# Padded sampled tiles and a moved feature sum in the gated recurrence of a one-core decoder kernel

## The chip, the cores and the metric

The kernel runs on one core of a Trainium2 chip. The metric is the device time of one execution in microseconds. Three executions of the kernel before took 2487.93, 2488.98 and 2489.5 us, so the median is 2488.98 us. TensorE (PE in the rows) multiplies, VectorE (DVE) and ScalarE (ACT) do elementwise work, GpSimd (POOL) only makes constants here, and SyncE (SP) issues most DMAs.

## The reference

A decoder trunk of two layers runs over 512 prompt tokens and 64 sampled tokens (8 sequences of 8). Layer 0 mixes with a gated linear recurrence of 8 heads with a 128 x 128 state each; layer 1 mixes with a diagonal state-space layer. Gated feed-forward blocks stand before and after each mixer. Cut to the recurrence:

```python
proj = h @ w_in                       # q, f, i, g of 1024 features each
fg = lbf + (1 - lbf) * sigmoid(f);  log_f = log(fg);  k = (1 - lbf) * sigmoid(-f)
# per token and head: S_t = diag(f_t) S_(t-1) + k_t v_t^T,  o_t = S_t^T q_t
o, s_T = chunk_scan(heads(q), heads(k), heads(i), heads(log_f), s0)
o = o * rsqrt(mean(o * o, axis=-1) + EPS) * gnorm
return (o * silu(g)) @ w_out, s_T
```

## The kernel before

All activations lie with features on the 128 partitions and the 576 tokens (512 prompt, then 64 sampled) along the row. A product of float32 quality is made of three products, h_hi w_hi, h_lo w_hi and h_hi w_lo, each in two halves of 288 tokens (line 1687). The halves w_hi and w_lo are made on ScalarE (`split`, line 657) and on VectorE (`rest`, line 1024).

The recurrence is the phase `hgrn_in`. It goes head by head; a step of the program projects head n and, between those matmuls, works on head m = n - 1. The 32 blocks of six matmuls that project head n are cut at the numbers in `cuts`, and after each cut stands a piece of head m. The pieces, in the order of TensorE, are:

- eight levels (0 to 7) of score matmuls. `level` multiplies k by q for four prompt tiles of 128 tokens (line 1822, a float32 matmul is two instructions in the trace) and, for levels 0 to 3, for the 64 sampled tokens (line 1824, 64 columns of k). VectorE's `level` multiplies q, k and the decay row (lines 1381 to 1383), which releases TensorE's next level, and then copies the scores under a mask (lines 1389 and 1393). Even levels use bank 4 of PSUM, odd ones bank 5, the sampled parts banks 6 and 7;
- `v_turned`, behind level 4, and `k_turned`, three blocks behind level 7: five transposes each into banks 6 and 7 (line 1657), copied by ScalarE to `v_tok` and `k_tok` (lines 803 and 804);
- `chunk_adds`, the k v products of the four chunks (line 1849), which VectorE's `chain` turns to the chunk states (lines 1411 and 1417);
- `tail`, behind the last block: sampled k v products, 64 rows deep and 512 columns wide, into banks 6 and 7 (line 1857); the prompt outputs in bank 5 (lines 1864 and 1866); the sampled outputs in bank 4 (line 1868, 64 rows deep, and line 1871, eight matmuls 8 columns wide); and last the sum over features of the squared outputs (line 1878), which needs ScalarE's squares (lines 830 and 831) in the tile `sq`.

ScalarE takes the root of those sums (line 833), VectorE inverts it in four quarters (`invert`, line 1443) in the next step, and `normalise` (line 1449) and `o_rest` (line 1454) finish the output of that head. VectorE also scales the projections as they leave PSUM (line 1050 by way of `scaled`), and adds the sampled k v products to the decayed states (line 1427) and gates the outputs (lines 1433 and 1435, which end with the semaphore `on_done`). Each engine runs its queue in program order; semaphores alone connect them. The last step projects no head: the first blocks of the phase `hgrn_out` stand between its levels, two behind each of the first six cuts.

## Time and profile before

| what | value |
|---|---|
| median of three executions | 2488.98 us |
| the profiled execution, its own time | 2480.59 us |
| its span, first to last instruction | 2478.8 us |
| TensorE busy | 2337.1 us (94%) |
| VectorE busy | 1220.8 us (49%) |
| ScalarE busy | 701.8 us (28%) |
| mean granted TensorE clock | 0.975 |
| DMA | 211.08 MB, mean 85 GB/s |

The profiled execution is 8.4 us (0.34%) shorter than the median of the three timed ones, and its span is 1.8 us shorter than its own time. Busy time counts an engine's instructions; TensorE's are pipelined, so that neighbouring rows overlap, and the distance between starts tells what one costs. An arrow in a row names what released the instruction after an idle stretch.

### The profile page before, as it was taken

The numbers are of one execution on the slowest core, as the hardware profiler recorded it, in microseconds if no ns is written. First come the engines' busy times: TensorE is split into PE (matmuls) and PEld (weight loads), VectorE is DVE, ScalarE is ACT, GpSimd is POOL, SyncE is SP. The second block draws the span as 40 slices with busy tenths as digits, with TensorE's granted clock in tenths as the row PEclk, the third lists the DMA queues.
The fourth block names the chain that finished last, engine by engine and source line by source line (L and its number), as shares of the span: only waits on it lengthen the run. The fifth ranks groups of instructions, "written<-read, shape, count | busy, mean of one in ns | idle before, by whom it ended". The sixth has DMA issues, their size and how long they took to land.

```text
span 2478.8 us, 42614 instructions
## 1 busy us (share of the span) xinstructions
PE 2337.1 (94%) x17438; PEld 2294.5 (93%) x17438; DVE 1220.8 (49%) x1730; ACT 701.8 (28%) x878; POOL 2.7 (0%) x15
## 2 busy tenths in 40 slices
PE   6999999899999979999999999999955999999998
PEld 6999999889999879999999999999945999999998
DVE  5755544756667665432344443243377434433333
ACT  3222222334434333221222322122234432221223
POOL 0000000000000000000000000000000000000000
PEclk9999999999999999999999999999967999999999
DMA  4223432432231115323422332322333233223322
GB/s 125 82 65 109 122 85 64 121 108 70 73 84 52 44 53 135 96 69 93 113 80 85 89 85 64 105 69 66 87 107 102 74 85 86 80 73 84 85 70 70
DMA packets 398495, 211.08 MB, mean 85 GB/s; under 512 B 23025, under 2 KB 393922, under 8 KB 398402
## 3 DMA queue, kind: packets, MB, share of 16 engines
q1 hardware_dynamic: 387666, 198.03, 28.8%
q10 hardware_dynamic: 10736, 11.77, 1.5%
q8 instruction: 63, 1.03, 0.2%
q14 instruction: 30, 0.25, 0.0%
HBM read 193.01 MB, written 20.94 MB: 86 GB/s over the span
## 4 chain that ended last, share of the span: by engine, by line
PE 87%; DVE 7%; issue 2%; ACT 2%; DMA 0%; ACTq 0%; SPq 0%; DVEq 0%
PE ps L1687 78%; PE ps L1822 2%; PE ps L1657 2%; DVE rstd L1045 1%; PE ps L1857 1%; PE ps L1871 1%; PE ps L1986 1%; PE ps L1987 1%; DVE w_lo L1024 0%; ACT w_hi L657 0%; PE ps L1878 0%; PE ps L1765 0%; DVE sq L1547 0%; PE ps L1864 0%; DVE sq L1550 0%
## 5 line engine op out<-in xcount | busy, mean ns | idle before, releaser
L1687 PE MATMUL ps<-h_hi,w_hi 128*128 128x288 f32 x3328 | 723.4, 299 | 14.5 <-DVE t_a L1050 11.6
L1687 PE MATMUL ps<-h_hi,w_lo 128*128 128x288 f32 x3328 | 713.9, 296 | 0.0
L1687 PE MATMUL ps<-h_lo,w_hi 128*128 128x288 f32 x3328 | 713.5, 296 | 0.0
L1687 PEld LDWEIGHTS ps<-h_hi,w_hi 128*128 128x128 f32 x3328 | 536.6, 189 | 20.2 <-issue 6.5
L1687 PEld LDWEIGHTS ps<-h_hi,w_lo 128*128 128x128 f32 x3328 | 537.4, 189 | 0.0
L1687 PEld LDWEIGHTS ps<-h_lo,w_hi 128*128 128x128 f32 x3328 | 537.3, 189 | 0.0
L1024 DVE TENSOR_TENSOR w_lo<-w_raw,w_hi 128x2048 fp32r<-128x2048 f32 (+3 forms) x184 | 369.8, 2010 | 123.8 <-ACT w_hi L657 122.1
L657 ACT ACTIVATE w_hi<-w_raw 128x2048 fp32r<-128x2048 f32 (+3 forms) x184 | 309.5, 1682 | 216.8 <-PE ps L1687 204.6
L1687 PE MATMUL ps<-g_hi,w_hi 128*128 128x288 f32 x1408 | 304.7, 298 | 0.0
L1687 PE MATMUL ps<-g_lo,w_hi 128*128 128x288 f32 x1408 | 303.2, 297 | 0.0
L1687 PE MATMUL ps<-g_hi,w_lo 128*128 128x288 f32 x1408 | 303.0, 297 | 0.0
L1050 DVE TENSOR_TENSOR t_b<-ps,rstd 128x576 f32<-128x576 f32 x88 | 66.6, 757 | 435.9 <-PE ps L1687 435.9
L1687 PEld LDWEIGHTS ps<-g_hi,w_hi 128*128 128x128 f32 x1408 | 228.7, 190 | 0.0
L1687 PEld LDWEIGHTS ps<-g_hi,w_lo 128*128 128x128 f32 x1408 | 228.6, 190 | 0.0
L1687 PEld LDWEIGHTS ps<-g_lo,w_hi 128*128 128x128 f32 x1408 | 228.5, 190 | 0.0
L723 ACT ACTIVATE g_hi<-t_g 128x576 f32 (+1 forms) x88 | 60.3, 685 | 527.4 <-DVE t_g L1283 527.4
L1328 DVE SCALAR_TENSOR_TENSOR x<-ps,x 128x576 f32<-128x576 f32 (+1 forms) x72 | 54.5, 757 | 247.9 <-PE ps L1687 247.8
L720 ACT ACTIVATE t_s<-t_a 128x576 f32<-128x576 f32 x88 | 60.3, 686 | 326.9 <-DVE t_a L1050 326.9
L1285 DVE TENSOR_TENSOR g_lo<-t_g,g_hi 128x576 f32 (+1 forms) x88 | 66.7, 758 | 79.8 <-ACT g_hi L723 79.8
L1050 DVE TENSOR_TENSOR t_a<-ps,rstd 128x576 f32<-128x576 f32 x88 | 66.2, 752 | 21.8 <-PE ps L1687 21.8
L688 ACT ACTIVATE h_hi<-x,vec 128x576 fp32r<-128x576 f32 (+1 forms) x40 | 31.0, 775 | 153.2 <-DVE x L1328 93.0
L1283 DVE TENSOR_TENSOR t_g<-t_b,t_s 128x576 f32<-128x576 f32 x88 | 66.8, 759 | 15.2 <-DVE t_b L1050 12.0
(301 smaller groups left out, 1860.5 us busy)
## 6 DMA issues: line engine op xcount, KB each, us to landing
w_raw<-in_ffn_w_in_dram SPq DMA_DIRECT2D x176, 512.0 KB, 4.8
w_raw<-in_ffn_w_out_dram SPq DMA_DIRECT2D x64, 384.0 KB, 3.7
w_raw<-in_ffn_w_out_dram SPq DMA_DIRECT2D x64, 320.0 KB, 3.4
w_raw<-in_hgrn_w_in_dram SPq DMA_DIRECT2D x32, 512.0 KB, 5.3
w_raw<-in_s_w_glu_dram SPq DMA_DIRECT2D x16, 512.0 KB, 4.7
wb_d<-wb_st ACTq DMA_DIRECT2D x8, 512.0 KB, 2.7
wc_d<-c_pow ACTq DMA_DIRECT2D x8, 512.0 KB, 3.5
s_in<-in_state_hgrn_dram SPq DMA_DIRECT2D x8, 512.0 KB, 3.9
```

Source lines behind the costliest of these rows:

```text
L657: nc.scalar.activation(w_hi[j][:, 0:ph.size], w_raw[j][:, 0:ph.size], ACT.Copy).then_inc(w_hi_done[j], 1)
L688: nc.scalar.activation(cols(h_hi, m), cols(x, m), ACT.Copy, scale=vec[:, bass.ds(m + gain, 1)])\
L720: nc.scalar.activation(t_s[:], t_a[:], ACT.Silu).then_inc(silu_done, 1)
L723: nc.scalar.activation(cols(g_hi, i * 2 + j), t_g[:], ACT.Copy).then_inc(g_hi_done, 1)
L1024: V.tensor_tensor(w_lo[j][:, 0:n], w_raw[j][:, 0:n], f32(w_hi[j][:, 0:n]), ALU.subtract)\
L1050: return V.tensor_tensor(halves(dst), pair(s), halves(rstd[:]), ALU.mult)
L1283: V.tensor_tensor(t_g[:], t_b[:], t_s[:], ALU.mult).then_inc(g_full, 1)
L1285: V.tensor_tensor(cols(g_lo, i * 2 + j), t_g[:], f32(cols(g_hi, i * 2 + j)), ALU.subtract)\
L1328: V.scalar_tensor_tensor(out=halves(cols(x, m)), in0=pair(j), scalar=scale, in1=halves(cols(x, m)), op0=ALU.mult, op1=ALU.add).then_inc(fr ...
L1657: return M.transpose(out, t, ident[0:n, 0:n])
L1687: ins = M.matmul(ps[:, 2 * s + h, 0:HALF], w[j][:, at:at + P], v[:, k, h * HALF:(h + 1) * HALF], start=k == 0 and n == 0, stop=k == ph.kt ...
L1822: ins = M.matmul(ps[:, 4 + n % 2, at], k_t[b][:, at], q_t[b][:, at], start=True, stop=True)
```

## The change

Four tiles get 128 entries where they had 64 for the sampled tokens: `k_t` and `v_t` are 640 wide with zeros in the last 64 columns, `own_seq` and `v_seq` have 128 rows. With them every matmul and transpose on sampled tokens uses 128 rows and 128 columns of weights: the sampled scores, the fifth transpose, the sampled k v products and the first sampled output. ScalarE copies both transposed banks in one instruction of 640 columns. The sampled k v products move from the tail to just behind `chunk_adds`. The feature sums of a head move from the end of its tail to behind level 4 of the next head; `v_turned` moves from behind level 4 to behind level 5, and waits for the root of those sums. On ScalarE the root of the head before stands behind the two sigmoids of the next step instead of ahead of the weight split. On VectorE the first inverted quarter moves from behind level 1 to behind level 5, and the second from behind level 4 to behind the scaling of v. Level 0 of the next head waits for `s_out_done` (line 1427's) instead of the root.

```diff
-    own_seq = sb("own_seq", [SAMPLE, DEC_BATCH])
+    own_seq = sb("own_seq", [P, DEC_BATCH])
...
-    k_t = [sb(f"k_t{b}", [P, T]) for b in range(2)]
+    k_pad = [sb(f"k_t{b}", [P, T_PAD]) for b in range(2)]
+    k_t = [k[:, 0:T] for k in k_pad]
...
-    v_seq = sb("v_seq", [SAMPLE, DEC_BATCH, P])
+    v_seq = sb("v_seq", [P, DEC_BATCH, P])
...
...
-                    nc.scalar.activation(dst[:, 0:CHUNKS, :].rearrange("p c q -> p (c q)"), ps[:, 6, :], ACT.Copy)
-                    nc.scalar.activation(dst[0:SAMPLE, CHUNKS, :], ps[0:SAMPLE, 7, 0:P], ACT.Copy).then_inc(done, 1)
+                    turned_both = ps[:, 6:8, :].rearrange("p b q -> p (b q)")[:, 0:T_PAD]
+                    nc.scalar.activation(dst[:].rearrange("p c q -> p (c q)"), turned_both, ACT.Copy).then_inc(done, 1)
...
-                    act.wait_ge(r_full, m + 1)
+
+                def head_root(head):
+                    act.wait_ge(r_full, head + 1)
                     nc.scalar.activation(halves(sq[:]), ps[:, 6:8, 0:HALF], ACT.Sqrt, scale=1.0 / P, bias=eps_t[:])\
...
+                    if n is not None:
+                        project_f(n, b)
+                    if before is not None:
+                        head_root(before)
...
...
-                    invert(before, 0)
                     if n is not None:
                         rest(ph, 1, n)
...
-                    invert(before, 1)
-                    if m is not None:
                         level(m, mb, 5)
+                    invert(before, 0)
...
                         take(v_t[:], 0, n, 1)
+                        invert(before, 1)
                         if last:
                             rest(PH[n_ph + 1], 0, 0)
...
+                    if n is None:
+                        invert(before, 1)
                     invert(before, 2)
...
...
-                            pe.wait_ge(osd_done, m)
+                            pe.wait_ge(s_out_done, m)
...
-                        ins = M.matmul(ps[0:SAMPLE, 6 + n % 2, 0:SAMPLE], k_t[b][:, SEQ:T], q_t[b][:, SEQ:T],
+                        ins = M.matmul(ps[:, 6 + n % 2, 0:SAMPLE], k_pad[b][:, SEQ:T_PAD], q_t[b][:, SEQ:T],
...
-                    turn(ps[0:SAMPLE, 7, 0:P], t[:, SEQ:T]).then_inc(done, 1)
+                    turn(ps[:, 7, 0:P], t[:, SEQ:T_PAD]).then_inc(done, 1)
...
+                    if not isinstance(m, int) or m:
+                        pe.wait_ge(osd_done, m)
+                    turned(v_pad, vt_full)
...
-                        ins = M.matmul(ps[:, 6 + h, :], k_tok[0:SAMPLE, CHUNKS, :], v, start=True, stop=True)
+                        ins = M.matmul(ps[:, 6 + h, :], k_tok[:, CHUNKS, :], v, start=True, stop=True)
...
-                    M.matmul(ps[:, 4, 0:SAMPLE], v_tok[0:SAMPLE, CHUNKS, :], score[0:SAMPLE, SEQ:T], start=True, stop=False)
+                    M.matmul(ps[:, 4, 0:SAMPLE], v_tok[:, CHUNKS, :], score[:, SEQ:T], start=True, stop=False)
...
-                    pe.wait_ge(osq_done, m + 1)
-                    pe.wait_ge(s_out_done, m + 1)
+                def sums(count):
+
+                    pe.wait_ge(osq_done, count)
+                    pe.wait_ge(s_out_done, count)
...
-                            if at == SAMPLE_LEVELS:
+                            if at == SAMPLE_LEVELS and (not isinstance(m, int) or m):
+                                pe.wait_ge(sc_read, m * LEVELS + SAMPLE_LEVELS)
+                                sums(m)
+                            if at == SAMPLE_LEVELS + 1:
                                 v_turned(m)
...
                                 chunk_adds(m)
+                                sampled_adds(m)
...
+                sums(HEADS)
```

Three places of the engines' order are shown, of a step in the loop over heads. First VectorE, from the mask copy of level 6 to the inversion behind level 7, before:

```order
L1389 COPY_PREDICATED score<-masks,ps 128x512
L1398 REGISTER_ALU
L1050 TENSOR_TENSOR v_t<-ps,rstd 128x576
L1022 REGISTER_ALU
L1024 TENSOR_TENSOR w_lo_56<-w_raw_52,w_hi_54 128x2048
L1363 REGISTER_ALU
L1381 TENSOR_TENSOR q_t_99<-q_t_99,e_t 128x4x64
L1382 TENSOR_TENSOR k_t_101<-k_t_101,e_t 128x4x64
L1383 TENSOR_TENSOR e_t<-e_t 128x4
L1389 COPY_PREDICATED score<-masks,ps 128x512
L1443 RECIPROCAL o_rs<-sq 128x144 x2
```

And the same stretch now (v scaled by line 1058, `rest` in line 1032, the level in lines 1391 to 1399, `invert` in line 1454):

```order
L1399 COPY_PREDICATED score<-masks,ps 128x512
L1409 REGISTER_ALU
L1058 TENSOR_TENSOR v_t<-ps,rstd 128x576
L1454 RECIPROCAL o_rs<-sq 128x144
L1030 REGISTER_ALU
L1032 TENSOR_TENSOR w_lo_56<-w_raw_52,w_hi_54 128x2048
L1373 REGISTER_ALU
L1391 TENSOR_TENSOR q_t_99<-q_t_99,e_t 128x4x64
L1392 TENSOR_TENSOR k_t_101<-k_t_101,e_t 128x4x64
L1393 TENSOR_TENSOR e_t<-e_t 128x4
L1399 COPY_PREDICATED score<-masks,ps 128x512
L1454 RECIPROCAL o_rs<-sq 128x144 x2
```

One inversion of 128x144 now stands between the scaling of v and the weight remainder w_lo, and so ahead of the multiplications of level 7.

Second TensorE, the end of a step, from the last projection row to the end of the tail, before (line 1857 the sampled adds, 1878 the feature sums):

```order
L1687 MATMUL ps<-h_lo,w_hi_55 128x288 x2
L1687 MATMUL ps<-h_hi,w_lo_57 128x288 x2
L1857 MATMUL ps<-v_seq,k_tok 128x512 x2
L1864 MATMUL ps<-score,v_tok 128x128 x2
L1866 MATMUL ps<-q_t_98,s_chunk 128x128
L1864 MATMUL ps<-score,v_tok 128x128
L1866 MATMUL ps<-q_t_98,s_chunk 128x128
L1864 MATMUL ps<-score,v_tok 128x128
L1866 MATMUL ps<-q_t_98,s_chunk 128x128
L1868 MATMUL ps<-score,v_tok 128x64
L1871 MATMUL ps<-q_t_98,s_in_115 128x8 x8
L1878 MATMUL ps<-sq,ones 128x288 x2
```

Now the sampled adds (line 1871) follow the chunk adds (line 1863), two blocks earlier:

```order
L1699 MATMUL ps<-h_hi,w_lo_57 128x288 x2
L1863 MATMUL ps<-v_tok,k_tok 128x128 x4
L1871 MATMUL ps<-v_seq,k_tok 128x512 x2
L1699 MATMUL ps<-h_hi,w_hi_55 128x288 x2
L1699 MATMUL ps<-h_lo,w_hi_55 128x288 x2
```

The tail now begins behind the last projection row and ends without the sums:

```order
L1699 MATMUL ps<-h_hi,w_lo_57 128x288 x2
L1880 MATMUL ps<-score,v_tok 128x128 x2
L1882 MATMUL ps<-q_t_98,s_chunk 128x128
L1880 MATMUL ps<-score,v_tok 128x128
L1882 MATMUL ps<-q_t_98,s_chunk 128x128
L1880 MATMUL ps<-score,v_tok 128x128
L1882 MATMUL ps<-q_t_98,s_chunk 128x128
L1884 MATMUL ps<-score,v_tok 128x64
L1887 MATMUL ps<-q_t_98,s_in_115 128x8 x8
```

The sums stand behind level 4 of the next head (line 1896), with the second weight tile's blocks behind them:

```order
L1829 REGISTER_ALU
L1834 MATMUL ps<-q_t_99,k_t_101 128x128 x4
L1896 MATMUL ps<-sq,ones 128x288 x2
L1692 REGISTER_ALU
L1699 MATMUL ps<-h_hi,w_hi_55 128x288 x2
L1699 MATMUL ps<-h_lo,w_hi_55 128x288 x2
```

Third ScalarE, from the gate's silu of one step to the sigmoid of the next, before (root in line 833, weight split in line 657):

```order
L797 ACTIVATE s_g_102<-pre 128x576
L830 ACTIVATE sq<-ps 128x512
L831 ACTIVATE sq<-ps 128x64
L833 ACT_TABLE_LOAD
L833 ACTIVATE sq<-ps,eps_t 128x576
L657 ACTIVATE w_hi_55<-w_raw_53 128x2048
L789 ISA
L790 ACT_TABLE_LOAD
L790 ACTIVATE k_t_101<-pre 128x576
```

And the start of a step now (sigmoids in lines 793 and 796, root in line 838, the copy of the transposed v in line 807):

```order
L793 ACTIVATE k_t_100<-pre 128x576
L795 ISA
L796 ACTIVATE f_t<-pre 128x576
L838 ACT_TABLE_LOAD
L838 ACTIVATE sq<-ps,eps_t 128x576
L807 ACTIVATE v_tok<-ps 128x640
L659 ISA
L660 ACTIVATE w_hi_54<-w_raw_52 128x2048
L815 ACTIVATE v_seq<-v_tok,own_seq 128x128 x8
```

The root with its table load stands between the second sigmoid and the copy of the transposed v.

## Rows read from the trace of the kernel before

**Rows 1.** The page: the chain that ended last, share of the span by engine.
```profile
PE 87%; DVE 7%; issue 2%; ACT 2%; DMA 0%; ACTq 0%; SPq 0%; DVEq 0%
```

**Rows 2.** Windows over two heads: engine busy times, granted clock, DMA share.
```profile
678.00:767.00 89.00, 87.02 (x644) 81.72 (x644) 59.95 (x112) 35.59 (x66) 0.00 (x0) 1.00 0.26 72
```

**Rows 3.** Waits from 500 to 900 us: total, times, longest.
```profile
ACT k_tok L803 <- PE ps L1657: 38.3, 8, 5.8
...
PE ps L1878 <- ACT sq L831: 6.4, 8, 0.8
...
PEld ps L1857 <- issue: 5.1, 23, 0.2
```

**Rows 4.** Timeline of TensorE, end of a head: start, length, instruction; next head's sums.
```profile
715.68 0.43 PE L1687 MATMUL ps<-h_hi,w_lo 128*128 128x288 f32 x2
716.04 1.98 PE L1857 MATMUL ps<-v_seq,k_tok 64*128 64x512 f32 x4
...
720.07 1.95 PE L1871 MATMUL ps<-q_t,s_in 128*128 128x8 f32 x16
722.83 1.24 PE L1878 MATMUL ps<-sq,ones 128*128 128x288 f32 x4 [0.80 <-ACT sq L831]
...
724.16 0.42 PE L1687 MATMUL ps<-h_lo,w_hi 128*128 128x288 f32 x2
...
767.14 1.24 PE L1878 MATMUL ps<-sq,ones 128*128 128x288 f32 x4 [0.80 <-ACT sq L831]
```

**Rows 5.** Timeline of TensorE, level 0 with and level 5 without sampled scores.
```profile
726.27 1.05 PE L1822 MATMUL ps<-q_t,k_t 128*128 128x128 f32 x8
727.25 0.33 PE L1824 MATMUL ps<-q_t,k_t 128*64 128x64 f32 x2
...
727.88 0.42 PE L1687 MATMUL ps<-h_lo,w_hi 128*128 128x288 f32 x2
...
745.80 1.05 PE L1822 MATMUL ps<-q_t,k_t 128*128 128x128 f32 x8
...
746.96 0.43 PE L1687 MATMUL ps<-h_lo,w_hi 128*128 128x288 f32 x2
```

**Rows 6.** Transposes of v by form, and TensorE's timeline of level 4 around them.
```profile
L1657 PE MATMUL ps<-ident,v_t x40: 272/273/273, 565.6 to 872.7; 128*128 128x128 f32 x32, 128*64 128x128 f32 x8
...
741.98 1.05 PE L1822 MATMUL ps<-q_t,k_t 128*128 128x128 f32 x8
...
743.68 0.30 PE L1687 MATMUL ps<-h_lo,w_hi 128*128 128x288 f32 x1
```

**Rows 7.** Timeline of VectorE around the tail and level 7, and TensorE's transpose of k.
```profile
723.57 0.27 DVE L1435 SCALAR_TENSOR_TENSOR ssq<-ps,vec,s_g 128x64 f32<-128x64 f32 x1
...
755.32 0.16 DVE L1383 TENSOR_TENSOR e_t<-e_t 128x4 f32<-128x4 f32 x1
...
756.01 1.95 DVE L1443 RECIPROCAL o_rs<-sq 128x144 f32<-128x144 f32 x2
...
755.64 0.71 PE L1657 MATMUL ps<-ident,k_t 128*128 128x128 f32 x5
```

**Rows 8.** Timeline of ScalarE: squares, table load, root, second sigmoid.
```profile
722.55 0.22 ACT L831 ACTIVATE sq<-ps 128x64 f32<-128x64 f32 x1
722.79 1.28 ACT L833 ACT_TABLE_LOAD   x1
...
724.10 0.74 ACT L833 ACTIVATE sq<-ps,eps_t 128x576 f32<-128x576 f32 x1
...
743.63 0.67 ACT L793 ACTIVATE f_t<-pre 128x576 f32<-128x576 f32 x1
```

**Rows 9.** Timeline of the last head, TensorE and VectorE.
```profile
866.76 0.53 PE L1687 MATMUL ps<-o_hi,w_hi 128*128 128x288 f32 x2 [1.12 <-DVE w_lo L1024]
...
884.89 0.35 DVE L1417 SCALAR_TENSOR_TENSOR s_end<-s_chunk,e_t,ps 128x128 f32<-128x128 f32 x1
...
885.39 0.68 PE L1864 MATMUL ps<-score,v_tok 128*128 128x128 f32 x4
```

More of the change, by code:

```diff
@@ L39 @@
 HALF = T // 2
+T_PAD = SEQ + P
 BANK = 512
@@ L202, in build_trunk @@
     q_t = [sb(f"q_t{b}", [P, T]) for b in range(2)]
-    k_t = [sb(f"k_t{b}", [P, T]) for b in range(2)]
+    k_pad = [sb(f"k_t{b}", [P, T_PAD]) for b in range(2)]
+    k_t = [k[:, 0:T] for k in k_pad]
     s_g = [sb(f"s_g{b}", [P, T]) for b in range(2)]
     f_t = sb("f_t", [P, T])
-    v_t = sb("v_t", [P, T])
+    v_pad = sb("v_t", [P, T_PAD])
+    v_t = v_pad[:, 0:T]
     pre = sb("pre", [P, T])
@@ L811, in own_values @@
                     for s in range(DEC_BATCH):
-                        ins = nc.scalar.activation(v_seq[:, s, :], v_tok[0:SAMPLE, CHUNKS, :], ACT.Copy,
+                        ins = nc.scalar.activation(v_seq[:, s, :], v_tok[:, CHUNKS, :], ACT.Copy,
                                                    scale=own_seq[:, s:s + 1])
@@ L824, in decayed, with squares @@
                     ins.then_inc(decay_done, 1)
-                def tail(m):
+                def squares(m):
                     act.wait_ge(o_full, m + 1)
@@ L848, in step @@
                             split(ph, 1, n, ph, n - 1)
-                        project_f(n, b)
                     elif m is not None:
                         split(PH[n_ph + 1], 1, 0, ph, None)
+                    if n is not None:
+                        project_f(n, b)
+                    if before is not None:
+                        head_root(before)
                     if m is not None:
@@ L870, in step @@
                     if m is not None:
-                        tail(m)
+                        squares(m)
                 step(0, 0, None, None, None)
@@ L1357, in hgrn @@
                 reciprocal(1)
+                for t in (k_pad[0], k_pad[1], v_pad):
+                    V.memset(t[:, T:T_PAD], 0.0)
                 link(V.memset(score[:], 0.0))
@@ L1392, in level @@
                     if n < SAMPLE_LEVELS:
-                        ins = V.copy_predicated(score[0:SAMPLE, SEQ:T], masks_s[:, n, :], ps[0:SAMPLE, 6 + n % 2, 0:SAMPLE])
+                        ins = V.copy_predicated(score[0:SAMPLE, SEQ:T], masks_s[:, n, :],
+                                                ps[0:SAMPLE, 6 + n % 2, 0:SAMPLE])
                     ins.then_inc(sc_read, 1)
@@ L1835, in v_turned @@
                     pe.wait_ge(sc_read, m * LEVELS + SAMPLE_LEVELS)
-                    turned(v_t, vt_full)
+                    if not isinstance(m, int) or m:
+                        pe.wait_ge(osd_done, m)
+                    turned(v_pad, vt_full)
                 def k_turned(m, b):
@@ L1841, in k_turned @@
                     pe.wait_ge(vtok_done, m + 1)
-                    turned(k_t[b], kt_full)
+                    turned(k_pad[b], kt_full)
                 def chunk_adds(m):
@@ L1850, in chunk_adds, with sampled_adds @@
                     ins.then_inc(kvp_full, 1)
-                def tail(m, b):
+                def sampled_adds(m):
                     pe.wait_ge(vseq_done, m + 1)
@@ L1856, in tail @@
                         v = v_seq[:, 4 * h:4 * h + 4, :].rearrange("p b v -> p (b v)")
-                        ins = M.matmul(ps[:, 6 + h, :], k_tok[0:SAMPLE, CHUNKS, :], v, start=True, stop=True)
+                        ins = M.matmul(ps[:, 6 + h, :], k_tok[:, CHUNKS, :], v, start=True, stop=True)
                     ins.then_inc(kvs_full, 1)
+                def tail(m, b):
                     pe.wait_ge(sc_read, m * LEVELS + LEVELS)
```

## The prediction

> **What bounds the kernel now.** I read the page first: TensorE is on 87% of the chain that ended last [rows 1], in a span of 2478.8 us (the table above). So only what shortens TensorE's own queue, or a wait of it, counts. The windows over two heads of the recurrence show TensorE busy 87.02 of 89 us at a full granted clock of 1.00, VectorE 59.95 and ScalarE 35.59 [rows 2]: here, too, TensorE is the bound, and its stalls are few but repeated, once or more in each period of 44.31 us (two starts of the feature sums) [rows 4]. The waits name them: 8 times TensorE waits for the squares before the feature sums, and 23 times its weight loads sit idle around line 1857 with no engine named ("issue") [rows 3]. The timeline then gives their price.
>
> The unit of price: 16 projection matmuls stand between 724.16 [rows 4] and 726.27 [rows 5], 0.132 us each. Level 5 takes 1.16 us from its first matmul to the second pair of projections [rows 5]; less two projections that is 0.112 us for each of its eight instructions.
>
> **The change, part by part**
>
> *Sampled scores, levels 0 to 3.* Level 0 takes 1.61 us on the same measure, 0.45 more than level 5, for two instructions with 64 columns of weights [rows 5]. At the pace above two would cost 0.22. With all 128 columns of weights I take 0.22, because 16 matmuls of line 1871 with full weights and only 8 moving columns keep about the same pace (1.95 us for all) [rows 4]. Saved: 0.23 a level, 0.9 a head. Bounds: nothing, or the whole 0.45 were the two free.
>
> *Sampled k v products and first sampled output.* From 715.68 to 720.07 stand two projections, four of line 1857, fourteen of lines 1864 and 1866 and two of line 1868: 4.39 us [rows 4]. Without a gap: 0.26, four at 0.43, sixteen at 0.112 (1.79), together 3.77. The 0.43 is an estimate by width: the sums of 288 columns take 0.24 each (below), 512 columns are 1.78 times that; the block's own 1.98 for four [rows 4] caps it at 0.5. Saved: 0.62, of which about 0.4 lies at line 1857 and 0.23 at line 1868. With the levels, 1.55 a head. That line 1857 now stands two blocks earlier is free: it needs the copy of k, for which `chunk_adds` waits anyway, and the eight copies to `v_seq`, and ScalarE, done with those, was idle until the transposed k came, 38.3 us in eight heads [rows 3].
>
> *Transposes.* Eight of the 40 for v have 64 columns of weights. Level 4 with its five transposes takes 1.70 us, 0.54 more than level 5, or 0.109 for each, the narrow one included [rows 5, 6]. Nothing to save. The Trainium skill, page "TensorEngine Tiling (Array Packing)", section "Key Properties", says that changing the tiling mode drains the engine. The score rows agree with it; the transpose rows don't show it, and the measurement decides. By the rule the 16 narrow transposes would save about 0.23 each, 3.7 us more.
>
> *The feature sums.* From 720.07 to 724.16 is 4.09 us [rows 4]; with projections directly behind the tail it would be 16 x 0.112 + 2 x 0.132 = 2.05. So 2.04 leaves the tail. In place the four sums take 1.07 (722.83 to 724.16 less two projections), the restart after the wait included [rows 4]. Without about 0.1 for the restart that is 0.24 each; behind level 4 I take 1.0, between 0.97 and 1.07. Their input is ready 20 us before (the squares end at 722.77, level 4 at 742.9) [rows 6, 8], and the wait for the mask copy of level 3 stood at the same spot before, ahead of the transposes of v, without idle time.
>
> *What now follows the tail.* Level 0 waits for `on_done`. It comes at 723.84, 3.77 us after 720.07 [rows 4, 7]. Level 0 would start 16 x 0.112 + 18 x 0.132 = 4.17 us after it: 0.4 to spare, so no stall in the loop. In the last step only 12 projections stand there, 3.37 us, so it waits about 0.5.
>
> *The root.* On ScalarE it now follows the second sigmoid, which ends at 744.30, 2.32 us after level 4 starts at 741.98 [rows 6, 8]. The table load takes 1.28, and the root 0.74 [rows 8]: finished 4.4 after the start of level 4. TensorE reaches the transposes of v after 0.9 + 1.0 + 18 x 0.132 + 0.9 = 5.2. It is hidden, with 0.8 to spare. The chip shows no more than the load itself: the square ends at 722.77, the load starts at 722.79 and ends at 724.07, the root starts at 724.10 [rows 8]. The Trainium skill, "ScalarE: Activation LUTs", section "What ACT_TABLE_LOAD costs", adds a drain of 1.38 us to the load; by that the root would come 0.6 us late.
>
> *The inversions, the cost of the change.* One quarter takes 0.98 us (1.95 for two) [rows 7]. The first, now behind level 5, falls into idle time of VectorE. The second stands ahead of the weight remainder and of level 7's multiplications. Those end at 755.48, and TensorE's transposes of k, which wait for them, start at 755.64 [rows 7]. There is at most 0.16 us of slack. With 0.98 more ahead, TensorE waits about 0.9, plus some hundredths for a first matmul after idle time: I take 0.94, between 0.8 and 1.1. Behind it, chunk adds, VectorE's chain and the tail shift together. VectorE's chain is still in time for the tail: in the last head, with no projections between, it ends 0.15 ahead of it (885.24 against 885.39) [rows 9], and in the loop two blocks of projections, 1.6 us, stand there as cover.
>
> *The sum.* Heads 1 to 6, one period each: 1.55 + 2.04 - 1.0 - 0.94 = 1.65, six times 9.9 us. Head 0 has no earlier head, so no sums and no inversions in it: 1.55. The last head gains 1.15 (levels and first output), 1.54 at its start (2.04 for the sums gone, 0.5 for the wait for `on_done`), and about 0.55 of the wait of 1.12 for w_lo, since an inversion no longer stands ahead of it [rows 9]. Against that the chain of VectorE decides: its slack was 0.15. It gets 0.46 later by the sums less the transposes moved, 0.98 by a third inversion behind level 7, and by an estimated 0.3 for the first behind level 5, the part that idle time does not cover: 1.6 after the slack. Net 1.65 for the last head. The last feature sums stay exposed. Sum: 9.9 + 1.55 + 1.65 = 13.1 us. The profiled execution would go from 2480.6 to 2467.5; it stands 8.4 us under the median of the runs, so I take the gain from the median: 2489.0 - 13.1 = **2475.9 us**. The mask tiles, the zero fills (three memsets before the first head) and the copy of 640 columns in one are worth less than 0.5 us in all, off the chain.
>
> **The rivals**
>
> *No stall at the transposes of k* (10%): if the weight remainder or the multiplications get their place earlier than I see, for instance because VectorE's scaling of v comes earlier in the step. For it: VectorE is idle a third of the time. Against: its stretch from v to level 7 is dense. Time: 6 x 0.94 = 5.6 less, 2470.3.
>
> *The narrow transposes pay a gap of their own* (3%): 16 of them at the 0.23 of a score level, 3.7 us more saved, 2472.2. Against it stands the pace of 0.109. That is what the Trainium skill's tiling page (above) implies.
>
> *The root comes late* (6%): if a switch of tables in mid-queue costs twice the load's 1.28, TensorE waits 0.5 (1.28 less the 0.8 to spare) and a restart of 0.1, six times: 3.6 us, 2479.5. Against it the 0.03 us between load and root. The drain on the Trainium skill's page on ScalarE would be such a second cost.
>
> *The padding does nothing* (8%): the gaps come from something other than the 64-wide form, a change of bank or of source. Then 1.55 is lost seven times and 1.15 once, 12.0 us: 2487.9, no change. Against it: line 1871 and line 1868 write the same bank and the gap stands between them all the same.
>
> *Slower* (5%): the root is now waited for in three queues, by TensorE ahead of the transposes of v, by ScalarE's copies behind it, by VectorE's inversion ahead of the gates. Each microsecond beyond the 0.8 to spare costs six. To lose over 0.2% (5 us) it must first eat 13.1, so it decides from 18.1 / 6 + 0.8 = 3.8 us late. At 4.5 us late: 2475.9 + 6 x 3.7 = 2498. Against it: the sigmoids end 2.3 us behind the start of level 4 now, and nothing new stands ahead of them.
>
> **How the numbers follow.** The forecast has 68%. A measurement of this kernel can tell about 0.2% from no change, 5 us. The forecast and the first three rivals are faster by more (87%), the padding rival is the same (8%), the last slower (5%). The forecast's own bounds are 0.8 to 1.1 for the stall (1.8 us over six heads), 0.97 to 1.07 for the sums (0.6) and 1 us for the last head: 2474 to 2478. The range reaches from the first rival to beyond the late root, with the 0.3% between profile and median in mind: 2470 to 2482 (it leaves out the last two).
>
> **What would show it.** In the profile after: a period of 42.66 us between heads where two starts of line 1871's block or of the sums stand 44.31 apart now; no "issue" waits at the sampled adds; the sampled score pair at 0.22; no idle time at the sums; a new wait of TensorE, transposes of k for VectorE's e_t, of about 0.9 us, six times; none at the transposes of v. Wrong would be: waits for the root at the transposes of v, a wait at level 0 for the gated outputs in the loop, or a granted clock under 1.00 in the recurrence.

## The result, and the profile after

| | median | range | executions | profiled execution | its span |
|---|---|---|---|---|---|
| before | 2489.24 us | 2487.93 to 2491.3 | 4 | 2480.59 us | 2478.8 us |
| changed | 2468.94 us | 2468.46 to 2469.75 | 4 | 2469.75 us | 2468.0 us |

The ratio is 0.9918 (95% interval 0.9904 to 0.9932): the changed kernel is 0.8%, 20.3 us, faster. Forecast were 2475.9 us and a range from 2470 to 2482, so the kernel came out 7.0 us below the forecast and 1 us below the range. The direction was right, the size too small.

The page of the changed kernel, busy times and the chain that ended last (to be read beside the table of before and [rows 1]):

```profile
PE 2327.8 (94%) x17438; PEld 2294.4 (93%) x17438; DVE 1220.7 (49%) x1733; ACT 702.0 (28%) x862; POOL 2.8 (0%) x15
...
PE 86%; DVE 8%; issue 3%; ACT 2%; DMA 0%; ACTq 0%; SPq 0%; DVEq 0%
```

TensorE still bounds the kernel, busy 9.3 us less; VectorE and ScalarE have the work that they had. Where the bound lost time is seen in its waits. This is TensorE in the loop over heads of the changed kernel, from 560 to 840 us (line waited at, releaser: total, times, longest). It is the only wait there:

```profile
PE ps L1669 <- DVE e_t L1393: 3.2, 5, 0.7
```

And the same view from 840 to 900 us, the last head and what follows it (left out: two waits of line 1699's products, for o_lo and w_lo):

```profile
...
PE ps L1834 <- DVE e_t L1393: 1.5, 2, 1.1
PE ps L1669 <- DVE e_t L1393: 0.9, 1, 0.9
PE ps L1863 <- ACT k_tok L807: 0.9, 1, 0.9
PE ps L1896 <- ACT sq L834: 0.8, 1, 0.8
PE ps L1834 <- DVE ssq L1446: 0.2, 1, 0.2
```

In the loop the six waits for the squares are gone (8 in all in [rows 3], one is left, after the last head), and the new wait that was forecast stands there, transposes of k for VectorE's e_t. The row gives 0.64 us each, idle time behind modelled ends of matmuls; by starts it costs 0.86 (`inv_behind`, below). It comes five times, not six, because the last step of the loop has only half a weight remainder ahead of level 7 (VectorE's line 1032 with 1024 columns in 1.16 us, in the other steps 2048 in 2.23). There is no wait at the transposes of v, so the root is never late, and none at level 0 inside the loop.

One sign that was forecast did not come. The weight loads of the sampled adds still sit idle with no engine named, 4.4 us in 16 times from 500 to 900 us, where [rows 3] have 5.1 in 23. So that row was not the price of the 64-wide form:

```profile
PEld ps L1871 <- issue: 4.4, 16, 0.5
```

The timeline of TensorE in one head of the changed kernel shows the pieces (start, length, instruction):

```profile
693.18 1.05 PE L1834 MATMUL ps<-q_t,k_t 128*128 128x128 f32 x8
694.07 1.14 PE L1896 MATMUL ps<-sq,ones 128*128 128x288 f32 x4
694.83 0.64 PE L1699 MATMUL ps<-h_hi,w_hi 128*128 128x288 f32 x2
695.31 0.42 PE L1699 MATMUL ps<-h_lo,w_hi 128*128 128x288 f32 x2
...
698.33 0.71 PE L1669 MATMUL ps<-ident,v_t 128*128 128x128 f32 x5
...
707.56 0.43 PE L1699 MATMUL ps<-h_hi,w_lo 128*128 128x288 f32 x2
708.61 0.77 PE L1669 MATMUL ps<-ident,k_t 128*128 128x128 f32 x5 [0.62 <-DVE e_t L1393]
...
711.69 1.88 PE L1871 MATMUL ps<-v_seq,k_tok 128*128 128x512 f32 x4
713.01 0.83 PE L1699 MATMUL ps<-h_hi,w_hi 128*128 128x288 f32 x2
713.68 0.42 PE L1699 MATMUL ps<-h_lo,w_hi 128*128 128x288 f32 x2
...
715.00 0.61 PE L1880 MATMUL ps<-score,v_tok 128*128 128x128 f32 x4
...
716.73 1.90 PE L1887 MATMUL ps<-q_t,s_in 128*128 128x8 f32 x16
718.49 0.50 PE L1699 MATMUL ps<-h_hi,w_hi 128*128 128x288 f32 x2
...
720.95 1.05 PE L1834 MATMUL ps<-q_t,k_t 128*128 128x128 f32 x8
721.84 0.33 PE L1836 MATMUL ps<-q_t,k_t 128*128 128x64 f32 x2
...
722.33 0.42 PE L1699 MATMUL ps<-h_lo,w_hi 128*128 128x288 f32 x2
```

Level 0 takes 1.38 us from its first matmul to the second pair of projections, against 1.61 [rows 5]: 0.23 saved. The sums take 1.24 (694.07 to 695.31) less two projections, 0.98. The projections stand 1.76 us behind the start of line 1887's block, where in [rows 4] the sums follow it after 2.76. The sampled adds occupy 711.69 to 713.68 less two projections, 1.73 or four times 0.43; the fourteen instructions of the prompt outputs and the two of the first sampled output 715.00 to 716.73, 1.73.

ScalarE's timeline at the place of the moved root (the second sigmoid, the table load, the root, and the copy of the transposed v), to be read beside [rows 8]:

```profile
694.83 0.67 ACT L796 ACTIVATE f_t<-pre 128x576 f32<-128x576 f32 x1
695.52 1.28 ACT L838 ACT_TABLE_LOAD   x1
...
696.81 0.74 ACT L838 ACTIVATE sq<-ps,eps_t 128x576 f32<-128x576 f32 x1
...
699.23 0.71 ACT L807 ACTIVATE v_tok<-ps 128x640 f32<-128x640 f32 x1 [1.68 <-PE ps L1669]
```

The root ends at 697.55, 0.78 us ahead of the transposes of v. That is the 0.8 to spare of the forecast, with no second cost at the switch of tables: 0.02 us from sigmoid to load and 0.01 from load to root.

**The time, piece by piece.** I cut the span at S0 (the first matmul on the scores of head 0) and at the start of the last matmul of the sampled output of each head. The last column is a further execution of before, profiled later (below). Its own time, 2490.57 us, is that of an ordinary execution.

| piece, us | before, the profile of the forecast | changed | before, profiled again |
|---|---|---|---|
| start to S0 | 549.0 | 552.4 | 552.0 |
| head 0 | 39.8 | 38.2 | 39.8 |
| heads 1 to 6, six periods | 265.9 | 254.8 | 265.9 |
| last head | 34.45 | 32.9 | 39.8 |
| to the end | 1589.7 | 1589.7 | 1591.3 |
| span | 2478.8 | 2468.0 | 2488.8 |

The last matmuls of the last head can be read in the group of line 1887's matmuls of the changed kernel (instructions: shortest, median, longest ns, first and last start):

```profile
L1887 PE MATMUL ps<-q_t,s_in x128: 228/256/256, 588.9 to 878.3; 128*128 128x8 f32 x128
```

and in the same group of `before_again`:

```profile
L1871 PE MATMUL ps<-q_t,s_in x128: 256/256/277, 590.1 to 897.5; 128*128 128x8 f32 x128
```

Between the first two columns the recurrence is 14.3 us shorter (1.6 + 11.1 + 1.6), where 13.1 were forecast. Between the last two it is 19.6; the 5.3 us between these two numbers lie in the last head of before alone. That is most of the missing gain, and it is not in the change's sum but in its base.

### The profile page after: what moved, and what is told of

It is laid out like the page before. It is cut to its first block, busy times and chain, and to the rows that moved or that the text cites. A ratio compares the mean times of both kernels' runs of the same rounds, so it can differ in the third digit from the quotient of the medians.

```text
span 2468.0 us, 42601 instructions
## 1 busy us (share of the span) xinstructions
PE 2327.8 (94%) x17438; PEld 2294.4 (93%) x17438; DVE 1220.7 (49%) x1733; ACT 702.0 (28%) x862; POOL 2.8 (0%) x15
## 4 chain that ended last, share of the span: by engine, by line
PE 86%; DVE 8%; issue 3%; ACT 2%; DMA 0%; ACTq 0%; SPq 0%; DVEq 0%
PE ps L1699 78%; PE ps L1834 2%; PE ps L1669 2%; DVE rstd L1053 1%; PE ps L1871 1%; PE ps L1887 1%; DVE w_lo L1032 1%; PE ps L2009 1%; PE ps L2010 0%; ACT w_hi L660 0%; PE ps L1777 0%; DVE o_rs L1454 0%; DVE sq L1559 0%; DVE sq L1562 0%; PE ps L1896 0%
## 5 line engine op out<-in xcount | busy, mean ns | idle before, releaser
L2009 PE MATMUL ps<-wi,u_lift 128*72 128x128 f32 x128 | 28.2, 307 | 49.0 <-ACT s_v L952 28.5
```

The costliest lines, as they stand in the source:

```text
L2009: M.matmul(out, u_lift[:, G_CT * ct + g, :], wi[ct % 2][:, g], start=True, stop=False)
```

## The experiments

In all of them `ones` and `zero` are tiles that matmuls without use read: in kernels with `fill`, their result is overwritten, or they add a product with zeros to a bank, and no value of the output changes.

### The kernel before, again, with all padding alone, with the moves alone

`before_again` is the kernel before without an edit.

> The kernel before, unchanged, for the spans of its own executions. In the two traces the recurrence (first score level to the last sampled output) is 14.3 us shorter after the change, but the timed medians differ by 20.3 us, and the one profiled execution of before was 8.4 us under its timed ones. Theory A: the change is worth 14 us in the recurrence, and the rest is a part outside it that varied in the executions of before; then the spans of this kernel spread from about 2479 to 2488 us, and a trace of a longer one shows the recurrence unchanged at 340.2 us and the extra time elsewhere. Theory B: the recurrence itself usually takes some 6 us longer than the first trace showed: then a longer execution shows periods over 44.3 us.

Measured: 2489.43 us (ratio 1.0005, 0.9995 to 1.0015). Neither theory fits as it was written. The recurrence is longer, as theory B has it, but its periods are unchanged at 44.31 us: the last head took 39.8 us where the first profile had 34.45. The trace of `turn_only` (below), which differs from before by its narrow transposes alone, has the same last head, 39.76 us at a granted clock of 0.83. The windows over the last head and the 32 us behind it (busy times by engine, granted clock, DMA), in the first profile of before:

```profile
855.00:889.50 34.50, 28.77 (x202) 25.22 (x202) 22.41 (x48) 10.69 (x27) 0.00 (x0) 1.00 0.05 16
889.50:921.50 32.00, 22.30 (x138) 21.52 (x139) 17.78 (x22) 9.38 (x14) 0.00 (x0) 0.84 0.17 50
```

In `before_again`:

```profile
858.00:898.00 40.00, 34.23 (x202) 29.02 (x202) 22.57 (x48) 10.87 (x27) 0.00 (x0) 0.83 0.05 14
898.00:930.00 32.00, 23.06 (x128) 21.91 (x129) 17.21 (x22) 8.81 (x13) 0.00 (x0) 0.73 0.13 39
```

In the changed kernel:

```profile
845.60:878.50 32.90, 28.98 (x203) 25.44 (x202) 22.34 (x48) 10.44 (x24) 0.00 (x0) 0.95 0.06 16
878.50:910.50 32.00, 22.59 (x137) 21.79 (x137) 17.78 (x22) 9.10 (x14) 0.00 (x0) 0.79 0.16 48
```

The same 202 instructions of before are granted 1.00 in one execution and 0.83 in the other. The timeline of TensorE in `before_again` shows where:

```profile
879.40 1.16 PE L1822 MATMUL ps<-q_t,k_t 128*128 128x128 f32 x8 [0.94 <-DVE e_t L1383]
881.49 2.07 PE L1822 MATMUL ps<-q_t,k_t 128*128 128x128 f32 x8 [0.93 <-DVE e_t L1383]
884.49 1.33 PE L1657 MATMUL ps<-ident,k_t 128*128 128x128 f32 x5 [0.93 <-DVE e_t L1383]
...
888.67 3.78 PE L1857 MATMUL ps<-v_seq,k_tok 64*128 64x512 f32 x4
```

Level 6 (879.40) still takes 1.16 us. From level 7 (881.49) on the matmuls run at the lower of the two levels, 1.2 instead of 2.4 GHz: eight instructions in 2.07 us, and line 1857's block in 3.78 instead of 1.98 [rows 4]. What precedes is the stretch in which TensorE has no projections left and waits 0.9 us for VectorE ahead of levels 6 and 7. In the first profile the same waits stand in the same places, and level 7 takes 1.16 us.

`pad_only` has every padding of the diff, `own_seq`, `v_seq`, `k_pad`, `v_pad` and the copy in one, with the order of before. `move_only` has the order of the changed kernel, with all tiles of 64 as before (its sampled instructions keep the rows and columns that are taken away below).

```diff
 pad_only, against before
-    ins = M.matmul(ps[0:SAMPLE, 6 + n % 2, 0:SAMPLE], k_t[b][:, SEQ:T], q_t[b][:, SEQ:T],
+    ins = M.matmul(ps[:, 6 + n % 2, 0:SAMPLE], k_pad[b][:, SEQ:T_PAD], q_t[b][:, SEQ:T],
...
 move_only, against the changed kernel
-    ins = M.matmul(ps[:, 6 + h, :], k_tok[:, CHUNKS, :], v, start=True, stop=True)
+    ins = M.matmul(ps[:, 6 + h, :], k_tok[0:SAMPLE, CHUNKS, :], v, start=True, stop=True)
```

> All four tiles padded, all instructions in the order of before. Theory of the prediction: 0.9 us a head at the score levels, 0.4 at the sampled adds and 0.25 at the first sampled output: the period falls from 44.31 to 42.75 us, the time by about 12 us. Rival (the gaps belong to a change of bank or source, not to the 64-wide form): period 44.3, time as before.

> The order of after, the four tiles and their copies unpadded as before. Theory: the sums leave a wait of 1.04 us a head behind and the moved inversion makes a new one of 0.9 us, so the period stays near 44.2 us and the time falls by about 2 us, most of it at the last two heads. Rival: the new wait is smaller without the padding, since TensorE is slower by 0.9 us in levels 0 to 3, and the moves are worth 5 us or more.

Measured: `move_only` 2486.33 us (0.9991, 0.9981 to 1.0), its period 44.19 us as expected. `pad_only` 2484.99 us (0.9989, 0.9979 to 0.9998), and its period 44.4 to 44.6, not 42.75: missed. The windows of `pad_only` around the end of a head:

```profile
586.00:592.40 6.40, 5.60 (x38) 4.53 (x37) 2.22 (x3) 1.75 (x4) 0.00 (x0) 1.00 0.31 92
592.40:596.00 3.60, 3.60 (x14) 3.15 (x13) 0.70 (x2) 2.86 (x3) 0.00 (x0) 0.53 0.86 253
596.00:600.00 4.00, 4.00 (x34) 4.00 (x34) 1.50 (x3) 1.89 (x2) 0.00 (x0) 1.00 0.63 171
```

And its timeline of TensorE there:

```profile
589.38 1.90 PE L1876 MATMUL ps<-q_t,s_in 128*128 128x8 f32 x16
592.08 1.95 PE L1883 MATMUL ps<-sq,ones 128*128 128x288 f32 x4 [0.80 <-ACT sq L834]
...
594.30 0.68 PE L1692 MATMUL ps<-h_lo,w_hi 128*128 128x288 f32 x2
...
596.07 0.42 PE L1692 MATMUL ps<-h_hi,w_lo 128*128 128x288 f32 x2
```

Behind eight matmuls (sixteen instructions) of 8 moving columns and a wait of 0.80 us, the clock falls to half for about 3.5 us in each head. A pair of projections takes 0.68 instead of 0.42. That is what the padding had saved, given back. Against 2488.41 us of before on that chip, the moves alone are worth 2.1 us and the padding alone 3.4 of the 20. Set beside the changed kernel, `move_only` prices the padding in the order in which no such wait is left: the period goes from 44.19 to 42.60, 1.59 us, where 1.55 were reckoned.

The last head is slow in both. It takes 38.3 us in `pad_only`, at 0.82, and 37.9 in `move_only`:

```profile
854.70:892.60 37.90, 34.41 (x204) 29.14 (x203) 22.43 (x48) 10.65 (x26) 0.00 (x0) 0.82 0.05 14
```

So neither half of the change by itself takes the half clock out of the last head.

### The padding, with the wait filled

`pad_fill` puts four matmuls of 0.22 us into the wait of `pad_only`.

```diff
+                    fill(4, more)
                     pe.wait_ge(osq_done, m + 1)
```

> The padded tiles in the order of before, and in each head's tail, where TensorE waits for ScalarE's squares, four float32 matmuls of 128 columns (0.9 us) whose result nothing reads, into a free bank. Theory (the padding alone was eaten by TensorE's clock, which its trace shows at half for 3.4 us at the end of each head): with the wait filled the clock stays at full, the period falls from 44.5 to 42.75 us and the time to about 12 us under before. Rival (something else lengthens each head of the padded kernel by 1.8 us): the period stays at 44.5 us.

Measured: 2473.25 us (0.9932, 0.9915 to 0.9948). The window over one period of it:

```profile
592.00:635.00 43.00, 43.00 (x333) 41.61 (x331) 30.01 (x57) 17.55 (x31) 0.00 (x0) 1.00 0.27 76
```

The clock is whole, and the period 42.96 us: 1.35 less than before's 44.31, of 1.55 forecast for the padding. The fills fit into the wait, for the feature sums start 2.74 us behind the block of line 1884 here and 2.75 behind line 1871's in before. What is missing lies at level 3, 0.26 us: VectorE's multiplications, which have the first inversion and a weight remainder ahead of them in this order, now end just too late for it. So the padding does what was reckoned, and the half clock hid it. The moves, which take both the wait for the squares and this inversion out of the way, are what lets it be seen. The time fell by more than the 12 us expected, 16.8 us under the runs of before beside it (2490.01). Against the trace of `before_again`, 1.6 of it lie in head 0, 8.1 in the six periods, 2.9 in the last head (36.94 us, at 0.86) and 3.9 behind it.

### The narrow transposes alone

`turn_only` pads the fifth transpose and copies 640 columns in one, and nothing else.

```diff
-    turn(ps[0:SAMPLE, 7, 0:P], t[:, SEQ:T]).then_inc(done, 1)
+    turn(ps[:, 7, 0:P], t[:, SEQ:T_PAD]).then_inc(done, 1)
```

> Before with the fifth transpose alone padded to 128 columns, and the copy of both banks in one instruction of 640 columns. Prediction's reading of the rows: nothing to save, the period stays at 44.31 us. Rival (the narrow transposes pay a gap too): period 43.85 us. A single look, read by its period.

Measured, in a single execution: 2488.3 us, period 44.32 against 44.31. A 64-wide transpose among wide ones costs nothing here, and the rival that gave it 0.23 is refuted.

### The stall at the transposes of k

`inv_behind` is the changed kernel with the second inversion behind level 7, out of the way of the multiplications.

```diff
                         take(v_t[:], 0, n, 1)
-                        invert(before, 1)
...
                         level(m, mb, 7)
-                    if n is None:
-                        invert(before, 1)
+                    invert(before, 1)
```

> After, with VectorE's second inversion moved from ahead of the weight remainder to behind level 7. Theory: the wait of TensorE for the multiplications of level 7 (0.9 us, five heads) goes, and VectorE's chain still ends ahead of the tail: 4 to 5 us faster than after, period 41.7 us. Rival: the chain, with three inversions ahead of it, becomes what the tail waits for, and nothing is gained.

Measured: 2464.08 us (0.9905, 0.9888 to 0.9921), period 41.74 against 42.60. In the waits of its TensorE from 500 to 900 us the row on e_t keeps the last head's wait alone:

```profile
PE ps L1667 <- DVE e_t L1393: 0.9, 1, 0.9
```

So the stall costs 0.86 us a head (0.94 forecast) and the inversion ahead of level 7 is its cause. Its last head is longer, 34.0 us instead of 32.9, and the window on it has a granted clock of 0.90, with the eight instructions of line 1861's chunk adds in 2.07 us. By the ratios (0.9905 against 0.9918) the whole kernel gains about 3 us, not the 4 to 5 expected, and the two intervals overlap; the period is what shows the effect.

### What the last head of before costs at half clock

`before_fill` is the kernel before, with three matmuls of zeros (of 0.22 us each) ahead of levels 6 and 7, the transposes of k and the chunk adds of the last head only.

```diff
+                        if n is None and 6 <= at < 10:
+                            fill(3)
```

> The kernel before, with three float32 matmuls of zeros behind each of the last four cuts of the last head, added to an open sum, so that they change no value; they stand where TensorE waits 0.9 us for VectorE. Theory (in ordinary executions of before the last head runs half of its time at half clock, 39.8 us instead of 34.5): with those waits filled the last head takes 34 to 35 us and the time falls by 5 to 6 us, to about 2483. Rival: the last head is slow for the tail's narrow matmuls or for another reason, and the time stays at 2488.

Measured: 2480.13 us (0.9964, 0.995 to 0.9978), 9.9 us under the runs of before beside it (2490.01): more than expected, and about the time of the first profiled execution of before (2480.59). Its timeline of TensorE between levels 6 and 7:

```profile
879.91 0.83 PE L1775 MATMUL ps<-ident,zero 128*128 128x128 f32 x6
881.00 1.16 PE L1830 MATMUL ps<-q_t,k_t 128*128 128x128 f32 x8 [0.26 <-DVE e_t L1385]
```

The wait of 0.93 ahead of level 7 is now 0.26, with other work in it, and its eight instructions take 1.16 us instead of 2.07. The last head took 34.46, as in the first profile, and what follows it 1586.7 instead of 1591.3. So, trace against trace, 5.3 us of the gain lie in the last head and 4.6 behind it, where two traces of the changed kernel alone differ by 2.5 (1589.7 and 1587.2). The first is shown; of the second, no run tells how much is the fills' work.

`after_fill` makes the same edit in the changed kernel; `after_again` is that kernel without an edit, on the same chip.

> The changed kernel with matmuls of zeros in the waits of the last head (three behind each of the last four cuts), as in the filled kernel of before, where they were worth 9.9 us. Theory (the change already took the half clock out of the last head): 1 to 2 us faster than after, 2467 to 2468. Rival (after pays for the half clock like before): 5 us or more.

> The changed kernel once more, for a second trace of its last head and more executions. Theory: the median stays at 2469 with little spread, the last head takes 33 us nearly all at full clock. Rival (the first trace of after was lucky, as the first of before was): a last head of 36 us or more and executions up to 2475.

Measured: 2467.56 (0.9921, 0.9904 to 0.9937) and 2466.76 us (0.9916, 0.9899 to 0.9932), last heads 32.69 and 32.91. The fills bring nothing here, not even the 1 to 2 us expected. The timeline of the changed kernel's last head shows why. First the sampled adds and what follows them, in the changed kernel:

```profile
871.56 3.49 PE L1871 MATMUL ps<-v_seq,k_tok 128*128 128x512 f32 x4
874.89 0.61 PE L1880 MATMUL ps<-score,v_tok 128*128 128x128 f32 x4
```

And the same two in `after_shift` (below), whose last head has a clock of 1.00:

```profile
873.90 1.88 PE L1879 MATMUL ps<-v_seq,k_tok 128*128 128x512 f32 x4
876.99 0.68 PE L1888 MATMUL ps<-score,v_tok 128*128 128x128 f32 x4 [1.20 <-DVE s_end L1430]
```

The changed kernel has half clock too, in the sampled adds, 3.49 instead of 1.88 us. But at full clock TensorE waits there 1.20 us for the end of VectorE's chain of chunk states, so that the outputs start 3.09 us behind the adds instead of 3.33. (`after_fill` has that wait too, 1.21 us.) Here the half clock costs about 0.2 us, because it falls where VectorE is late in any case.

### Is it the design of the change, or the moment?

Each of these two has eight matmuls, 1.8 us, put ahead of the last head and is otherwise before or the changed kernel.

```diff
+                    if n is None:
+                        fill(8, True)
                     for at, cut in enumerate(cuts):
```

> The kernel before with eight float32 matmuls (1.8 us of dense work, result read by nothing) ahead of the last head's first block. If the length of the last head (39.8 us, half of it at half clock) hangs on when its thin stretch comes, it may fall to 34.5 plus 1.8 and the time falls by 3 us or more; if it hangs on how thin the stretch is, the time rises by 1 to 2 us.

> The changed kernel with the same eight matmuls ahead of its last head. They lie partly in the 0.5 us wait of the first level for the gated outputs. If the full clock of its last head is owed to the moment at which it comes, the last head may rise to 38 us and the time by 4 us or more; if it is owed to the change itself, the time rises by about 1.3 us.

Measured: `before_shift` 2485.19 us (0.9991, 0.9981 to 1.0), 3.4 us under the runs of before beside it (2488.60), its last head 36.23, that is 34.45 and the 1.8 added, at a granted clock of 1.00. `after_shift` 2470.99 us (0.9931, 0.9915 to 0.9948), its last head 33.98, at 1.00 too. So before keeps its full clock in this profile if the same waits come 1.8 us later, and the changed kernel's did not fall. Its time did rise by 4.2 us over `after_again`, which was the mark set for the other theory. But the last head has only 1.1 of that; between the two traces 1.1 lie ahead of the recurrence and 1.9 behind the last head, where no edit was made, and nothing here explains them.

`before_shift` says that the waits of the last head do not bring the half clock by their form alone. Whether it is the moment at which they stand, or the 1.8 us of dense work ahead, no run separates. The changed kernel had 0.95 in both of its traces, 1.00 when shifted and 0.90 with the inversion moved. With the order of the changed kernel and the narrow tiles (`move_only`), or the wide tiles and the order of before (`pad_only`), it was 0.82. Why it stays up when both are together is open.

### The version that follows

`best_fill` is `inv_behind` with the fills of the last head, four matmuls ahead of the last feature sums and 22 ahead of the output projection that waits for the last head's output.

```diff
+                        if k == HEADS - 1:
+                            fill(22)
                         pe.wait_ge(o_ready, k + 1)
...
                 step(None, 0, HEADS - 1)
+                fill(4)
                 sums(HEADS)
```

> The kernel with the second inversion behind level 7, and with matmuls of zeros in the waits of the last head, in its wait for the squares and in the wait of hgrn_out for the last head's output. Theory of the clock: the half clock from the end of the last head into hgrn_out goes, 13.7 us at half there cost up to 7 us, of which 4 to 6 come back: 2459 against 2464. Rival: the matmuls of zeros delay the levels by as much as the clock gives.

Measured: 2462.1 us (0.9889, 0.9873 to 0.9906), the fastest of all kernels, its last head 32.65 us at a granted clock of 1.00. It missed the 2459 expected: it stands 2 us from `inv_behind`, whose interval overlaps, and the clock in the 32 us behind the last head rose from 0.79 there to 0.89 only. Even the step from the changed kernel (0.9918, 0.9904 to 0.9932) to the moved inversion and the fills together has intervals that overlap a little, and is only tolerably clear.

## Why the forecast was right in its parts and wrong in its sum

**The sampled scores, the adds and the first output (1.55 a head).** Right: 0.23 a level, in `pad_fill` 0.40 at the adds and 0.29 at the first output, and head 0, in which nothing else shortens TensorE's queue, is 1.63 us shorter. The "issue" waits at the adds, which were read as the sign of this gap, stayed.

**The feature sums (2.04 out of the tail, 1.0 back in).** Right: 0.98 in place, no idle time at them, none at the transposes of v.

**The root.** Right to 0.02 us. The Trainium skill, "ScalarE: Activation LUTs", section "What ACT_TABLE_LOAD costs", would have a drain of 1.38 us beside the load; the rows of ScalarE above show none, so the measurement decides. The rival of a late root falls, and with it the slower one.

**The inversion (0.94 a head).** 0.86, shown by `inv_behind`, and five times instead of six: the last step of the loop was reckoned as an ordinary one. The period was forecast at 42.66 us and is 42.60; the six give 11.1 instead of 9.9, of which 0.9 is the sixth stall that does not come.

**The last head (1.65).** 1.56 against the profile from which it was worked out. Level 0 waits 0.20 instead of 0.5. VectorE's chain decides, as was reckoned: where the clock is full, TensorE waits 1.20 us for it. That the half clock of the sampled adds fits into this wait was not foreseen.

**The transposes.** Right to give them nothing. The Trainium skill, "TensorEngine Tiling (Array Packing)", section "Key Properties", says that a change of tiling mode drains the engine. The score rows agree (0.23 for each excursion), `turn_only` does not.

**The padding does nothing.** As a mechanism refuted by `pad_fill`. But `pad_only` is nearly that result, 3.4 us, by a cause that was not in the list of rivals: "a granted clock under 1.00 in the recurrence" stood there as a sign of error, not as a price. That sign also came in the changed kernel itself, 0.95 in the last head, and the forecast had no term for it.

**The step that failed** is the base: "it stands 8.4 us under the median of the runs, so I take the gain from the median". That treats the 8.4 us as lying outside what the change touches. For the larger part they do not: before's profile of an ordinary execution is 3.0 us longer ahead of the recurrence, 5.3 in the last head and 1.6 behind it. The 5.3 are TensorE at half clock. The 1.6 are less than the 2.5 by which two traces of one kernel differ there, so they have no cause shown. `before_fill` shows that the penalty is real: work that adds nothing takes 9.9 us off before's median. The changed kernel hardly pays it (32.9 us, 32.7 with the fills). So it has the 14.3 that its recurrence gained (13.1 forecast), the 5.3 of the last head and the 1.6 behind it, less 0.4 at the start: 20.8 us between the spans of the two ordinary executions, 20.3 between the medians. One profile could not say where the 8.4 us lie. But its last head had waits of 0.9 us and a clock of 1.00, and the 32 us behind it 0.84, so that the head might be slower in other executions was a term to be left open, with some 5 us downward in the range.

**Open:** why the clock in the changed kernel's last head stays up (0.95), when it does not with either half of the change alone (0.82). `before_shift` shows that 1.8 us ahead of the head can turn it, so this part of the gain, about 5 of 20 us, is not shown to be secured by the design of the change. Nor is it settled what makes the 3.0 us ahead of the recurrence: the window from 200 to 300 us has a granted clock of 1.00 in the first profile and 0.98 in `before_again` and in the changed kernel, which fits 2 of the 3, and no run looked further.

## What to carry to other kernels

A 64-wide matmul among 128-wide ones cost about 0.23 us for each excursion here, and zeros that fill it up were free; but one of two changes to the same spot can hide the other, as the padding gained 3.4 us alone and 16.8 once the wait behind it was filled (8.1 of that in the six periods). Where the profiled execution differs from the median, find the stretch in which it does before subtracting a gain from either. A wait of under a microsecond in a sparse stretch of TensorE can cost a few more behind it at half clock: read the granted clock by windows around such waits, and try matmuls of zeros in them. Look first whether another engine is late just behind: there the half clock costs little, and so do the fills gain little.

## What the runs showed of the hardware

- The same instructions in the same order took 34.5 or 39.8 us in one head, at a granted clock of 1.00 or 0.83, in two executions of one program (whether on one chip is not on record); with 1.8 us of matmuls ahead, the clock was 1.00 again (36.2 us).
- Eight matmuls with 8 moving columns (sixteen instructions) and a wait of 0.80 us were followed by about 3.5 us at half clock in `pad_only` (0.53 in the window), and not in before, where the same block and wait have the 64-wide instructions ahead. Four matmuls in the wait prevented it.
- Twelve useless matmuls, 2.7 us of TensorE's time, made the kernel before 9.9 us faster. In the changed kernel they made no difference (2467.56 against 2466.76 us): its half clock lay where TensorE would have waited for VectorE, 3.33 us between two starts instead of 3.09.
